# A down projection in seven products of quarters instead of 32 slabs, in a one-core encoder step

## The reference

```python
# mixer: conv module, banded attention, gated conv from one input projection
x = x + concat(rmsnorm(y_a), rmsnorm(o), rmsnorm(y_c)) @ w_out
x = x + cross_attention(rmsnorm(x), memory_k, memory_v) @ w_xo
x = x + square(relu(rmsnorm(x) @ w_up)) @ w_down      # 1024 -> 4096 -> 1024
```

## Time and profile before

| | us |
|---|---|
| median of 3 executions | 1726.28 (1724.88 to 1726.34) |
| the profiled execution, its own time | 1727.3 |
| its span in the profile | 1725.5 |
| PE busy | 1639.0 |
| DVE, ACT, POOL busy | 881.5, 588.4, 143.8 |
| DRAM traffic (packets in all) | 154.14 MB |

### The profile page before, as it was taken

The page is one execution under the profiler, slowest core; times in us unless marked ns, Lnnn a source line. Parts: engine busy times, 40 slices in busy tenths (PEclk is TensorE's granted clock), DMA queues, the critical chain, the costliest instruction groups (busy, mean ns, idle before and its releaser), DMA issues.

```text
span 1725.5 us, 25973 instructions
## 1 busy us (share of the span) xinstructions
PE 1639.0 (95%) x10788; PEld 1598.7 (93%) x10788; DVE 881.5 (51%) x1244; ACT 588.4 (34%) x984; POOL 143.8 (8%) x201
## 2 busy tenths in 40 slices
PE   6999999997888899998889989999999999999999
PEld 6999999995777899997779989999999999999999
DVE  6626776447889643244644375555555523223221
ACT  6511021136787432224532253333334311111100
POOL 1011000002220010002400000000001100000000
PEclk9999999987999999998989989999999999999999
DMA  7324111002110143101051222222223734141131
GB/s 270 106 84 167 37 37 37 25 10 87 36 35 25 61 164 130 37 13 50 29 174 69 85 76 106 110 105 108 102 101 138 243 131 153 37 153 44 43 101 53
DMA packets 44489, 154.14 MB, mean 89 GB/s; under 512 B 5088, under 2 KB 10648, under 8 KB 44240
## 3 DMA queue, kind: packets, MB, share of 16 engines
q0 software_dynamic: 20256, 80.70, 13.0%
q1 hardware_dynamic: 24128, 71.93, 12.3%
HBM read 116.82 MB, written 40.77 MB: 91 GB/s over the span
## 4 chain that ended last, share of the span: by engine, by line
PE 86%; DVE 6%; ACT 4%; issue 3%; DMA 1%; POOL 0%; SPq 0%; ACTq 0%; DVEq 0%; POOLq 0%
PE ps L442 33%; PE ps L2494 21%; PE ps L2467 18%; PE ps L2040 3%; PE ps L471 2%; PE ps L2369 2%; PE ps L2224 2%; PE ps L2337 1%; PE ps L2202 1%; PE ps L493 1%; ACT scores L1049 1%; DVE pt_lo L1648 1%; PE ps L2502 1%; PE ps L2186 1%; DVE scores L1627 1%
## 5 line engine op out<-in xcount | busy, mean ns | idle before, releaser
L442 PE MATMUL ps<-A_hi,w_hi 128*128 128x364 f32 x768 | 175.3, 337 | 0.0
L442 PE MATMUL ps<-A_lo,w_hi 128*128 128x364 f32 x768 | 172.0, 333 | 0.0
L442 PE MATMUL ps<-A_hi,w_lo 128*128 128x364 f32 x768 | 171.3, 332 | 0.0
L2019 DVE TENSOR_TENSOR Y<-ps,Y 128x1092 f32<-128x1092 f32 x31 | 40.2, 1296 | 245.0 <-PE ps L2494 233.7
L383 DVE TENSOR_TENSOR w_lo<-w_raw,w_hi 128x1024 fp32r<-128x1024 f32 x44 | 53.7, 1223 | 165.9 <-ACT w_hi L379 165.5
L442 PEld LDWEIGHTS ps<-A_lo,w_hi 128*128 128x128 f32 x768 | 136.3, 192 | 0.0
L442 PEld LDWEIGHTS ps<-A_hi,w_hi 128*128 128x128 f32 x768 | 135.8, 193 | 0.0
L442 PEld LDWEIGHTS ps<-A_hi,w_lo 128*128 128x128 f32 x768 | 135.5, 191 | 0.0
L379 ACT ACTIVATE w_hi<-w_raw 128x1024 fp32r<-128x1024 f32 x42 | 44.3, 1057 | 262.2 <-PE ps L442 156.7
L1309 ACT ACTIVATE w_hi<-w_raw 128x1024 fp32r<-128x1024 f32 x32 | 34.0, 1061 | 277.7 <-PE ps L2494 276.8
L2467 PE MATMUL ps<-t_hi,wq_hi 128*128 128x272 f32 x480 | 99.4, 288 | 0.8 <-DVE wq_lo L1930 0.8
...
## 6 DMA issues: line engine op xcount, KB each, us to landing
...
hid_d<-hid_stage POOLq DMA_DIRECT2D x30, 544.0 KB, 2.9
Y<-xT POOLq DMA_DIRECT2D x16, 546.0 KB, 4.8
y_d<-Y POOLq DMA_DIRECT2D x16, 546.0 KB, 3.1
Y<-y_d POOLq DMA_DIRECT2D x16, 546.0 KB, 4.1
hid_raw_b<-hid_d POOLq DMA_DIRECT2D x16, 544.0 KB, 5.4
hid_raw_a<-hid_d POOLq DMA_DIRECT2D x16, 544.0 KB, 6.5
...
```

Of the source, the lines that this page charges most:

```text
L442: ins = e.matmul(PS[:, 3 * par + c, 0:CH], wt[:, wpar, w], xt[:, col:col + CH], start=(first and n == 0 and m == 0), stop=(last and n == l ...
L2019: e.tensor_tensor(chunks(y(m)), ps_tile(d % 2), chunks(y(m)), ALU.add).then_inc(s.d_read, 1)
```

## The change

Line numbers in this section's listings of the change are those of the changed kernel.

1. **The down projection by seven products.** The weights are taken as 2 x 2 blocks A (hidden half by output parity), the hidden activations as 2 x 2 blocks B (hidden half by token half). Seven products of 16 steps each (`down(n)`); a step is one 128-channel slice of 4 output tiles by 544 tokens, 4 x 3 x 2 = 24 matmuls of 272 columns. A product runs in all eight PSUM banks; products whose contributions lie above each other go on accumulating, and after each product DVE adds four 544-column quarters to `Y` (`down_evac`, 28 additions in all).
2. **Its right operand.** Instead of whole hidden tiles, GpSimd stores quarters and their sums: per pair of tiles, seven DMAs of 272 KB (B11, B22, T1, T2, T3, B21, T4) and four subtractions of 544 columns. `hid_stage` is a single buffer, and `combine` waits for these. SP loads one quarter per step (`right_load`) into a ring of eight.
3. **Its left operand.** A11 is loaded by SP, A21 by GpSimd after product 104, in four loads of 1 MB each. GpSimd adds S1 = A21 + A22 (16 additions of 512 columns) with A22 streamed through `w_raw` in 512 KB halves; DVE makes the further sums (`down_sum`) for products 1, 2, 4 and 5. Products 3, 5 and 6 stream their block. The residual comes back in two groups of four tiles: before A21, and after S1.
4. **The two plain hidden tiles** go into `hid_stage` too, and through the same seven stores.
5. **Statistics.** In W_in, W_xq and up, the transposes stand behind the first half (36 matmuls) of tile 1, not ahead of it. In W_in, the eight memory-key transposes stand in the middle of tile 2.
6. **The start.** Weight slab 0 is loaded first, then the parameters and the memory; it is rounded in two halves. The loads of x wait for the second half of the memory. ACT loads its table ahead of the first data.

```diff
-S_DN = 94
-N_SLABS = 126
+KD = 16
+N_STEP = 7 * KD
...
+        RIGHT = (R_B11, R_T2, R_T3, R_T4, R_T1, R_B22, R_B21)
+        OUT = ((0, 0), (0, 1), (1, 1), (1, 0), (1, 1), (0, 1), (0, 0))
+        FIRST = (0, 4, 6)
+        SUMS = {1: 0, 2: 16, 4: 32, 5: 48}
+        STREAM = {1: (0, W_A22), 3: (8, W_A22), 5: (16, W_A12), 6: (24, W_A12)}
...
@@ sync @@
+            def right_load(n):
+                ii, k = divmod(n, KD)
+                if ii == 0:
+                    sp.wait_ge(s.b11_out, 16 * (k + 1))
+                if n >= 8:
+                    sp.wait_ge(s.d_step, n - 7)
+                sp.dma_start(down_right(2, n), rd[RIGHT[ii], k]).then_inc(s.r_in[n % 8], 16)
...
@@ gpsimd @@
-            def hid_store(p, half):
-                g.wait_ge(s.u_sq, 4 * p + 3 + half)
-                g.dma_start(hid_d[2 * p + 2 + half], HST[:, half]).then_inc(h_out[half], 16)
...
+            def quads(hp):
...
+                sq(3)
+                if hp:
+                    g.wait_ge(s.t_out0, 32 * hp)
+                    g.wait_ge(s.t_out12, 32 * hp)
+                g.tensor_tensor(TQ[0][:, :], b12, b11, ALU.subtract).then_inc(s.q_t, 1)
+                g.wait_ge(s.q_t, 4 * hp + 1)
+                g.tensor_tensor(TQ[1][:, :], b22, TQ[0][:, :], ALU.subtract).then_inc(s.q_t, 1)
+                g.tensor_tensor(TQ[2][:, :], b22, b12, ALU.subtract).then_inc(s.q_t, 1)
...
+            for m in (0, 2, 4, 6):
+                g.dma_start(y(m), y2_d[m]).then_inc(s.y2_back, 16)
+            g.wait_ge(s.sp_lo, N_PROD)
+            stream_load(g, 0)
+            stream_load(g, 1)
+            g.wait_ge(s.prod, N_PROD)
+            for z in range(4):
+                if z:
+                    g.wait_ge(s.a21_in, 16 * z)
+                g.dma_start(ZA21[z][:, :, 0:512], wdn[W_A21 * KD + 4 * z:W_A21 * KD + 4 * z + 4]
+                            .rearrange("k p c -> p k c")).then_inc(s.a21_in, 16)
+            for k in range(KD):
+                g.wait_ge(s.a21_in, 16 * (k // 4 + 1))
+                stream_wait(g, 1, k)
+                g.tensor_tensor(zone(ZS, k), zone(ZA21, k), stream_at(1, k), ALU.add).then_inc(s.s1_done, 1)
+                if k % 2:
+                    g.wait_ge(s.s1_done, k + 1)
+                    stream_load(g, 2 + k // 2)
...
@@ scalar @@
+            def down_hi(n):
...
+                e.activation(WQ[0][:, down_slot(n)], down_left(n), ACT.Copy).then_inc(s.d_whi, 1)
+                e.wait_ge(s.r_in[n % 8], 16 * (n // 8 + 1))
+                e.activation(down_right(0, n), down_right(2, n), ACT.Copy).then_inc(s.d_rhi, 1)
...
@@ vector @@
                 e.wait_ge(s.prod, q + 1)
-                if p:
-                    e.wait_ge(h_out[m], 16 * (p + 1))
+                e.wait_ge(s.q_t, 4 * p + {3: 1, 4: 3, 5: 3, 6: 4}[i])
+                if i != 5:
+                    e.wait_ge({3: s.b11_out, 4: s.b22_out, 6: s.b21_out}[i], 16 * (p + 1))
...
+            for n in range(4, N_STEP):
+                if n + 1 < N_STEP:
+                    down_sum(n + 1)
+                down_lo(n)
+                if n > KD and n % KD == 1:
+                    down_evac(n // KD - 1)
+            down_evac(6)
...
@@ tensor @@
+            def half_tile(half, i, X):
+                pe_part(e, i % 2, i % 2, X, range(4 * half, 4 * half + 4), first=half == 0, last=half == 1)
...
+            half_tile(0, 1, A)
             pe_bcast(e, cnt, crc, rc_wait(n_rc))
-            up(1)
+            half_tile(1, 1, A)
...
+            def down(n):
+                ii, k = divmod(n, KD)
+                e.wait_ge(s.d_wlo, n + 1)
+                e.wait_ge(s.d_rlo, n + 1)
+                for g in range(4):
...
+                    elif k == 0:
+                        e.wait_ge(s.d_read, 4 * (ii - 1) + g + 1)
+                    for m, (wx, xx) in enumerate(((0, 0), (0, 1), (1, 0))):
+                        for c in range(2):
+                            ins = e.matmul(PS[:, 2 * g + c, 0:HC], WQ[wx][:, down_slot(n), g * P:(g + 1) * P],
+                                           down_right(xx, n)[:, c * HC:(c + 1) * HC],
...
```

More of the change, by code:

```diff
@@ L223, in __init__, with build @@
         self.Q, self.KV = Q, KV
-def build(nc, xT, memT, slabs, params, rbrev, ctxa, ctxc, kcT, vc, mkcT, mvc,
+def build(nc, xT, memT, slabs, wdn, params, rbrev, ctxa, ctxc, kcT, vc, mkcT, mvc,
           o_y, o_ca, o_cc, o_k, o_v, o_kc, o_vc, o_mk, o_mv):
@@ new lines, in _ @@
+            for hp in range(KD):
+                quads(hp)
+            for q, v in ((s.b11_out, 16 * KD), (s.b21_out, 16 * KD), (s.b22_out, 16 * KD), (s.t_out0, 32 * KD),
+                         (s.t_out12, 32 * KD)):
+                g.wait_ge(q, v)
+            for m in (0, 2, 4, 6):
[4 more added lines that the diff above has]
+            g.wait_ge(s.prod, N_PROD)
@@ new lines, in _, with stores @@
+            g.wait_ge(s.y2_back, 64)
+            for m in (1, 3, 5, 7):
+                g.dma_start(y(m), y2_d[m]).then_inc(s.y2_back, 16)
+            def stores(ii):
+                for p in range(4):
+                    g.wait_ge(s.d_read, 4 * ii + p + 1)
+                    g.dma_start(o_quad(ii, p), y_quad(ii, p)).then_inc(s.stored, 16)
+            for m in range(10, 32):
+                ii, kp = {8: 3, 16: 5, 24: 6}[(m - 2) // 8 * 8], (m - 2) % 8
+                g.wait_ge(s.d_wlo, KD * ii + 2 * kp + 2)
+                stream_load(g, m)
+                if m == 17:
+                    stores(3)
+                if m == 18:
+                    stores(4)
+                if m == 26:
+                    stores(5)
@@ L865, in _ @@
+            g.wait_ge(s.stored, 16 * 12)
             for q, v in ((s.state_out, 96), (s.mem_stored, 32), (s.cache_out, 32), (s.kv_out, 128)):
@@ L1987, in _ @@
             relu_std(1)
-            for q in range(1, N_PROD):
+            for q in range(1, N_PROD + 4):
                 if q >= 4:
@@ L2511 @@
+            for n in range(N_STEP):
+                down(n)
+_INS = ["xT", "memT", "slabs", "wdn", "params", "rbrev", "ctxa", "ctxc", "kcT", "vc", "mkcT", "mvc"]
 _OUTS = {"o_y": (KT, P, T), "o_ca": (2, 2, P, CA), "o_cc": (2, 2, P, CC), "o_k": (4, P, 576), "o_v": (4, P, 576),
```

445 lines of the change are left out of this document (232 added, 213 removed).

## The result

The changed kernel takes **1700.65 us** (median of 4, 1695.06 to 1703.7), the kernel before 1726.31 on the same runs: ratio 0.9843, interval 0.9811 to 0.9875. So it is faster by 1.6% where 2.2% (1688) was forecast, inside the range of 1677 to 1703, near its upper end, and outside the forecast's own range of 1682 to 1696. The profiled execution has a span of 1700.0 us against 1725.5: 25.5 less, where the sum said 38.4.

A forecast was written before the change was run, and what follows sets the result against it. TensorE was taken as the bound: matmul count times time each, plus waits. From a 1725.5 us span, -44.9 (down projection), -4.0 (statistics), +10.5 (stall) gave 1687.1; +1.8 around it, -1.0 for the median: 1688, range 1677 to 1703.

The forecast's parts named there:

- The likeliest case: The forecast itself: 1688 us, with one PE gap at the end of product 0 of the down projection; chance 0.55.
- The tail: Behind the last down-projection matmul: a wider DVE addition and a larger last store, +0.4 us.
- the second rival: Down projection, product 1: GpSimd's S1 and DVE's sums exclude each other at every step, streams slow; 1699 to 1705, chance 0.15.
- the standing of DVE: Start of down product 1: DVE stands for about one GpSimd instruction in each of three rounds, +3 us.
- Where the stages meet: From product 104's end into down product 1: PE stalls 10.5 us, bounds 3 and 16.
- The loads: After product 104: A21's first megabyte lands at 32 us, the others about 6 each, S1 starts at 44.
- Up stage: costed at 0, at most 3: Up stage: GpSimd's four subtractions and seven stores per pair fit within the pair's 21.1 us; 0, at most 3.
- Statistics inside a tile: Half of tile 1 ahead of the transposes: W_in -1.3, W_xq -1.2, up -1.5; sum -4.0 us, bounds -2 and -7.
- the 6.95 us of 32 two-column matmuls stay: W_in: waits of 0.6 us go, but the small statistics matmuls still take 6.95 us.
- The slow tile: W_in: the tile behind the small statistics matmuls stays slow, 14.05 us against 12.01.
- the -1.5: Up tiles: product 1 starts at about 1024.5 instead of 1026.06, with DVE late next; -1.5 us.
- The start: 0 +- 1.5: Program start: slab 0 first and xT loads waiting leave the first statistics as before; 0, bounds +-1.5 us.

The follow-up runs named there:

- the interleaved kernel: Against the changed kernel, GpSimd makes S1 of each four steps once its megabyte of A21 is there, not after all four loads are issued; 1686.67 us.
- the experiment: Against the changed kernel, the three places where half of tile 1 runs ahead of the transposes are put back to the old order; 1713.52 us.

## Why the prediction was right or wrong

**Right in kind.** The gain is matmul counting: 2688 matmuls of 272 columns at 0.126 us. No stream, no right load and no product but the first held PE: after the gap, products 1 to 6 run as one piece. The likeliest case named the place (end of product 0), the releasers (DVE's lo, then its addition to Y), GpSimd's S1 behind them and the third megabyte of A21 behind that; all of it is in the rows. The tail was right to 0.1.

The time is nevertheless in the band of the second rival (1699 to 1705), and it is from there that the range had its upper end of 1703. Of that rival the standing of DVE is true, and with more effect than in the forecast. But it didn't hold for every step of product 1: behind the three rounds at its start and one more (1407.56 to 1414.19) DVE runs at 0.60 to 0.64 an instruction, PE waits for nothing, and the streams cost nothing.

**"Where the stages meet" was the mis-sized term: 10.5 forecast, 24.8 measured** (362.5 - 337.7), above the 16 of its bound. 18.9 are the two waits, some 4.1 the slower clock of 60 matmuls in and behind the gap (25 in 5.6 us, the next 35 in 6.0, where 0.1256 each is the full rate), 1.8 a slightly lower rate of the rest. Two of its steps failed:

- *The loads.* "z0 lands at 32, the others about 6 each, S1 starts at 44". It was 36.0, then 6.6 and 8.2, one issue more, and 51.5: 7.5 late. Of that 1.9 is GpSimd's own end (the first load of Y is issued at 16.9, not 15), 2.1 the way to z0, 2.8 the two chained megabytes and 0.7 the fourth issue. The first A21 load is issued only at 22.9, behind six issues of 0.5 to 0.8 and 2.5 us idle among them: the sum had bytes, and no time on the queue.
- *The standing of DVE.* "About one instruction of GpSimd's in each of the three rounds, +3." From S1's start to the first addition it was 17.2 us where the sum had 10.8; the excess over DVE's own work was 10.4, not 3. The 3.44 us rounding stands for two of GpSimd's instructions in a row, not one, for a reason that the rows don't show. In the interleaved kernel this was the larger part of 7.8 us, where the whole stall was forecast at 7.3.

**"Up stage: costed at 0, at most 3" was wrong by 5.1.** The reasons given held (no wait for `q_t` or a store, 17.2 of 21.1 us would do), but another wait was not seen: ACT's and DVE's lists put the rounding of the down stage's step 0 ahead of the last combinations, and it needs a megabyte that may only be issued after product 100 and takes 8 us. With the roundings put later the wait goes and the products take 313.6 us, as before. The prediction never asked what is queued behind that wait.

**"Statistics inside a tile": -4.0 forecast, -6.4 measured**; by the experiment they are worth some 8 to 11 (W_in 4.3 to 7.4, then 1.9 and 1.7). W_xq was short by 0.8. For W_in the step that failed is "the 6.95 us of 32 two-column matmuls stay": they became 4.49, and 3.46 in most kernels. The slow tile did stay in this profile (14.23 against 14.05). For up, the -1.5 became -0.3. The forecast had DVE late for product 1 and product 0 at full pace. Product 0 does start 1.6 us earlier within its stretch (130.15 us from W_xo's start, not 131.75), and the 0.8 of wait ahead of product 1 goes, but a wait of 5.6 us now stands right ahead of product 0, which then takes 5.2 us instead of 3.0. GpSimd's first sums are not what took it back, since putting them later changed nothing. Only without half tiles do they cost: there PE waits 2.3 us for product 1's rounding, where it waited 0.8 before.

**"The start: 0 +- 1.5"**: +2.4 in this pair of profiles, +1.1 as a mean over all.

**Cross-attention, -5.4, was not forecast** and could not be from the change: it is the granted clock in the same code, 0.92 over the stage against 0.84.

The two that were off by most, 14.3 and 5.1, were in part made up by 5.4 of the clock in cross-attention and 2.8 in W_in; the total misses by 12.9. The 5.4 is luck; as an estimate, 1700.65 + 5.4 = 1706 without it, above the range.
